# Sixteen cache copies moved among the weight pieces of the first stage of a hybrid decoder step

## What is computed

```python
u = x * (1 + sc1) + sh1
proj = u @ w_in                       # 1024 x 2560, float32
xa, ga, q, k, v = jnp.split(proj, [D_A, 2 * D_A, 2 * D_A + D_B, 2 * D_A + 2 * D_B], axis=-1)
y_a, new_conv, h_last = rglru_branch(xa, ga, ...)
q = rope(q.reshape(b, t, N_HEADS_B, HEAD_DIM), pos)
k = rope(k.reshape(b, t, N_HEADS_B, HEAD_DIM), pos)
...
k_all = jnp.concatenate([k_buf.astype(k.dtype), k], axis=1)      # the 8 sequences
v_all = jnp.concatenate([v_buf.astype(v.dtype), v], axis=1)
keep = min(WIN_MAX, k_all.shape[1])
new_k, new_v = k_all[:, -keep:], v_all[:, -keep:]
```

## Time and profile before

| | us |
|---|---|
| median of three runs | 1359.38 |
| lowest, highest | 1357.69, 1365.87 |
| profiled execution, span | 1363.8 |
| TensorE busy (PE) | 1196.5 (88%) |
| VectorE busy (DVE) | 735.4 (54%) |
| ScalarE busy (ACT) | 577.3 (42%) |

### The profile page before, as it was taken

How to read it: one execution, slowest core, us unless ns; L and a number is a source line. 1 busy time by engine, 2 the same in 40 slices (tenths; PEclk the granted TensorE clock), 3 DMA queues, 4 the chain that set the end, 5 groups by cost and what they waited for, 6 DMA issues and landing times. The chain is left out here.

```text
span 1363.8 us, 20897 instructions
## 1 busy us (share of the span) xinstructions
PE 1196.5 (88%) x6933; PEld 907.3 (67%) x6934; DVE 735.4 (54%) x1247; ACT 577.3 (42%) x845; POOL 137.3 (10%) x129
## 2 busy tenths in 40 slices
PE   5699899999699979969995389999999999999854
PEld 3699787877255647627783277777778877778721
DVE  3356534343356747527545775789641455476147
ACT  2556443111245644214233264677531454465124
POOL 0000000000000001002431200011000000000055
PEclk8799899999699999879997599999999999999977
DMA  9985931259669948877333596899661455597184
GB/s 333 368 289 195 354 126 64 70 179 333 242 206 352 307 134 273 272 208 233 126 119 130 183 335 261 324 380 399 232 234 62 138 215 210 214 371 268 38 342 178
DMA packets 102028, 316.94 MB, mean 232 GB/s; under 512 B 12845, under 2 KB 21533, under 8 KB 95290
## 3 DMA queue, kind: packets, MB, share of 16 engines
q1 hardware_dynamic: 85146, 273.97, 57.5%
q0 software_dynamic: 6432, 23.33, 4.8%
q10 hardware_dynamic: 10384, 18.76, 3.7%
HBM read 281.22 MB, written 101.93 MB: 281 GB/s over the span
## 5 line engine op out<-in xcount | busy, mean ns | idle before, releaser
L2584 DVE TENSOR_TENSOR e_downl<-e_wd,e_downh 128x1024 fp32r<-128x1024 f32 x64 | 74.1, 1220 | 65.3 <-ACT e_downh L2479 65.3
L2646 PE MATMUL e_psY<-e_downh,e_hTh 128*128 128x512 f32 x216 | 91.0, 421 | 15.7 <-DVE e_hTl L2605 14.5
L2479 ACT CAST e_downh<-e_wd 128x1024 fp32r<-128x1024 f32 x64 | 62.4, 1048 | 68.5 <-DMA e_wd<-in_w_exp_down 68.5
L552 PE MATMUL n_psA<-n_wh,u_h 128*128 128x512 f32 (+1 forms) x216 | 88.1, 408 | 0.4 <-DVE n_wl L811 0.4
L2646 PE MATMUL e_psG<-e_gateh,e_xTh 128*128 128x512 f32 x216 | 86.4, 400 | 2.0 <-DVE e_gatel L2578 2.0
L2646 PE MATMUL e_psG<-e_uph,e_xTh 128*128 128x512 f32 x216 | 87.8, 406 | 0.2 <-issue 0.2
L2648 PE MATMUL e_psG<-e_gatel,e_xTh 128*128 128x512 f32 x216 | 85.9, 398 | 0.0
L2647 PE MATMUL e_psG<-e_gateh,e_xTl 128*128 128x512 f32 x216 | 85.9, 398 | 0.0
L554 PE MATMUL n_psA<-n_wh,u_l 128*128 128x512 f32 (+1 forms) x216 | 85.8, 397 | 0.0
L2647 PE MATMUL e_psY<-e_downh,e_hTl 128*128 128x512 f32 x216 | 85.7, 397 | 0.0
L2648 PE MATMUL e_psY<-e_downl,e_hTh 128*128 128x512 f32 x216 | 85.5, 396 | 0.0
(11 more groups left out here) (406 smaller groups left out, 2573.0 us busy)
## 6 DMA issues: line engine op xcount, KB each, us to landing
e_wg<-in_w_exp_gate SPq DMA_DIRECT2D x16, 2048.0 KB
e_wu<-in_w_exp_up SPq DMA_DIRECT2D x16, 2048.0 KB
e_wd<-in_w_exp_down SPq DMA_DIRECT2D x16, 2048.0 KB, 14.4
out_k_s<-in_cache_win_k SPq DMA_DIRECT2D x8, 4088.0 KB, 21.1
out_v_s<-in_cache_win_v SPq DMA_DIRECT2D x8, 4088.0 KB, 34.5
a_wring<-in_w_ada SPq DMA_DIRECT2D x16, 1024.0 KB, 5.3
scratch_y<-e_y ACTq DMA_DIRECT2D x54, 256.0 KB, 4.3
n_wr<-in_w_in SPq DMA_DIRECT2D x20, 512.0 KB, 7.0
```

The lines of the kernel that those rows point to most:

```text
L552: nc.tensor.matmul(dst, lh, rh, start=(k == 0), stop=False)
L2479: nc.scalar.copy(w["down"][H_][:, k, :], ew["down"][:, k, :]).then_inc(s_dh.sem, s_dh.unit)
L2584: nc.vector.tensor_tensor(w["down"][L_][:, k, :], ew["down"][:, k, :], w["down"][H_][:, k, :], ALU.subtract).then_inc(s_dl.sem, s_dl.unit)
L2646: nc.tensor.matmul(dst, left[H_], right[H_], start=first, stop=False)
```

## The change

All sixteen copies are issued in `front`. One each stands behind p2, p3, p6, p8, p9, p10, p11, p12 and p13, two behind p5, four behind p15; the last one is issued once the nine k tiles are transposed, ahead of the small result writes as before. `attention` issues no copies and waits only for the two small writes of new rows. `finish` waits for 16 copies in place of 12.

```diff
-            finish(nc, a, out, dram, ident, route, tables, s_tables, s_cache, 12)
+            finish(nc, a, out, dram, ident, route, tables, s_tables, s_cache, 2 * B)
...
-    COPIES = (2, 3, 4, 5, 7, 8, 10, 11)
-    LAST = 4
+    COPIES = {2: 1, 3: 1, 5: 2, 6: 1, 8: 1, 9: 1, 10: 1, 11: 1, 12: 1, 13: 1, 15: 4}
+    LAST = 1
...
             for n in range(RAW, NPIECE):
                 load_piece(n)
-                if n in COPIES:
+                for _ in range(COPIES.get(n, 0)):
                     copy_cache(copied)
                     copied += 1
             sp.wait_ge(s_qt.sem, s_qt.at(NTT))
             for _ in range(LAST):
                 copy_cache(copied)
                 copied += 1
+            assert copied == 2 * B
...
-            def copy(b):
-                sp.dma_start(ov[b:b + 1, 0:PAST - TS, :], cv[b:b + 1, TS:PAST, :]).then_inc(s_cp.sem, s_cp.unit)
...
-            copy(CT)
-            copy(CT + 1)
             sp.wait_ge(s_mm.sem, s_mm.at(PIECES))
...
-            copy(CT + 2)
-            copy(CT + 3)
...
-            sp.wait_ge(s_cp.sem, s_cp.at(B - CT + 2))
+            sp.wait_ge(s_cp.sem, s_cp.at(2))
```

More of the change, by code:

```diff
@@ L1049, in attention @@
         turned = lambda s: 2 * chunk0[s]
-        cv = a["cache_win_v"].rearrange("b s h d -> b s (h d)")
         ok, ov = (out[n].rearrange("b s h d -> b s (h d)") for n in ("k_s", "v_s"))
```

## The result

The changed kernel takes 1367.71 us (median of 10 runs, 1363.65 to 1369.25), the kernel before 1361.55 us (median of 10 runs, 1350.12 to 1365.87). The medians lie 6.2 us apart. The ratio estimated from all the runs is 1.0056, 95% interval 1.0036 to 1.0076: 7.6 us slower (4.9 to 10.3), inside what the prediction called within 1%. The forecast was +1.6 us and 1361. The span of the profiled execution went from 1363.8 to 1367.5 us, +3.7.

What follows compares the result with a forecast made beforehand. TensorE, busy for 88% of the span, was taken to bound the kernel. The shift up to the squares +1.2, the expensive step +6.0 and the block end −5.6 gave +1.6 us on the median 1359.4: 1361.0 us, range 1353 to 1371.

Steps and rivals of the forecast that it cites:

- The block end: First stage's end: late copies delay the small result writes that TensorE's next block awaits; moving three copies earlier gives −5.6 us.
- The copies leave attention at no price: Attention stage: taking out its four 4 MB copies is worth 0, since nothing waits for them before 505.5.
- The landing of the weight pieces: First stage's DMA queue: p9 lands at 138.2, p11 at 165.1, p13 at 194.4, p16 at 265 (256.6 to 272.7).
- the second rival: First stage: V copies at 13.3 us and stores paid in full, p16 at 272.7, sum +9.3, 1368.7 us; chance 0.17.
- the third: First stage: V copies cost 14.6 us each, stores in full, p16 at 281.8, sum +18.4, 1377.8 us; chance 0.08.
- the K price with the stores in full: Queue up to p16: copies at 12.1 us each plus 7.7 us for stores, landing p16 at 264.3.
- The squares: Sum of squares before gate r3: TensorE waits until about 182.9, then 2 us of slow clock; shift up to here +1.2 us.
- i2's wait and its gain: Gate matmuls for channel block 2: p9 lands earlier, the wait goes, TensorE gains 7.4 us, which does not last.
- the chain: From p11's landing through ScalarE and VectorE to the sum of squares: moves by 0.3 us alone, TensorE starting 0.8 us earlier.
- The expensive step: Copies and stores ahead of p16: it lands at 265, TensorE stalls 4.0 us at the fifth k tile, plus 2 us half clock.
- A clock that stays up into attention is no rival: Block end into attention: the clock drops within the first microsecond after the last transposes, so a shorter gap gains nothing there.
- a shorter attention as a sign against itself: Attention from its first matmul (349.0 to 510.7) should stay unchanged; getting shorter without its copies would show the forecast wrong.

Runs made afterwards that it cites:

- the spread copies: Changed kernel with twelve copies in the first stage (none behind p10, two behind p15, none at the end) and four in attention: 1348.14 us, ratio 0.9907.

## Why the prediction was right or wrong, point by point

**The block end: right.** Foreseen −5.6 us, some 1.4 us left; the wait fell from 7.26 to 1.55, −5.7. The copies leave attention at no price, right too (157.9 us with four, 157.9 without, both with the same clock at the start).

**The landing of the weight pieces: right, all of them.** p9 foreseen at 138.2, taken at 138.92; p11 165.1, taken at 165.97; p13 194.4, taken at 194.81, and r3 did not wait for it; p16 at 265.0. The last was issued at 232.9:

```profile
L373 SPq DMA_DIRECT2D n_wr<-in_w_in x1: 374/374/374, 232.9 to 232.9; - x1
...
DMA to landing us min/median/max: 31.4/31.4/31.4
```

It landed at 264.3. So the copies cost 12 to 13.4 us each in the queue, and the second rival (the V price and the stores in full) and the third (dearer copies) did not come. What the 11 stores took from the queue is not told apart: 264.3 is also what the prediction has for the K price with the stores in full. The Trainium skill (DMA: Bandwidth & Descriptors, "Issuing engines are not separate DMA queues"), which the prediction held against the change, agrees with the trace in that the two queues share the engines (96 packets of each in 16 us); what that cost here was the latency of the stores, and the forecast asked only for their bytes.

**The squares: right place, one term too small.** i2's wait and its gain (7.4) went, the wait came at 183: foreseen until 182.9, measured until 183.81, the start of this line before (183.77). The slow clock behind it was charged 2.0 us; the row 183.81 alone takes 3.76 in place of 1.99, and the v matmuls run at half clock until 191.5. From the squares to r3 are 16.76 us after and 13.16 before: 3.6 us. The shift at r3 is +3.6, not +1.2: 0.9 from the chain, 1.6 from the clock. The price came from one row, that of i2 (1.95 us behind a wait of 5.47); at the two new waits it was 3.6 us behind 8.25 and 1.8 us behind 9.03, so one row was no bound for it.

**The expensive step: the failed one.** The prediction put the stall at the fifth k tile, behind p16's cast, 4.0 + 2 us. It came at the third, 9.03 us long, with 1.8 us of slow clock behind it (14.4 − 3.6 − 9.0), and by then p16's cast held nothing: ScalarE took p16 and p17 at 268.26, when the store had let TensorE go on; p16 had been there since 264.3 (232.9 + 31.4). The false step is the sentence that charges each v and k store "between 0 and 0.7 us". It asked what the stores take from the copies' queue, and not what the copies do to the stores: it had no landing time for a store and named nobody who waits for one. The wait was in the code, the third rotation waiting for the first store because ROT is 2; before, with landings of 2.0 us, it never showed in the trace. The runs with a third buffer and with 2 KB pieces show that the store is what TensorE waited for. The foreseen stall came only in the latter, where p16 was 6.4 us later still (270.7). With the landing and the shift that the changed kernel had, the prediction's own working gives it almost nothing: 264.3 + 6.0 = 270.3 for the rotated tile against 265.83 + 3.6 = 269.4 for TensorE, 0.9 us, and with a third buffer it was nil.

**"A clock that stays up into attention is no rival": wrong in this execution.** Granted clock in attention's first stretches, before and then after:

```profile
349.00:354.00 5.00, 2.73 (x12) 1.44 (x12) 1.36 (x9) 1.37 (x6) 1.39 (x3) 0.50 0.74 241
354.00:359.00 5.00, 4.23 (x16) 0.99 (x14) 2.90 (x12) 1.36 (x5) 0.00 (x0) 0.50 0.94 313
359.00:364.00 5.00, 5.00 (x25) 2.28 (x17) 0.88 (x3) 1.95 (x6) 0.00 (x0) 0.50 0.99 385
```

```profile
357.70:362.70 5.00, 2.03 (x12) 1.04 (x12) 1.36 (x9) 1.37 (x6) 1.40 (x3) 0.61 0.70 231
362.70:367.70 5.00, 4.18 (x17) 1.05 (x16) 2.90 (x12) 1.36 (x5) 0.00 (x0) 0.71 0.98 331
367.70:372.70 5.00, 5.00 (x40) 2.70 (x40) 2.88 (x9) 2.42 (x7) 0.00 (x0) 1.00 1.00 406
```

Before, the clock is at 0.50 for attention's first 15 us; after, it falls only behind the first matmuls (0.93 us in place of 1.65) and is back at 1.00 ten microseconds in: the 3.8 us. The prediction read 0.67 in the gap as what any gap does. But the shorter gap alone does not settle it: with the same 1.55 us, attention took 157.3 to 157.9 us in three of the profiles, 158.8 to 159.9 in four (one of these with 4.2 us for the late bias), and 161.0 with the spread copies. The first matmuls' row tells them apart: 0.93 us in the changed kernel, with a third buffer, with four copies back in attention (157.3 to 157.9) and with the small writes ahead (159.5); 1.11 with 2 KB pieces (158.8); 1.65, like the kernel before, without copies, with the copy behind p10 moved and with the spread copies (159.2 to 161.0). Why the clock falls ahead of the first matmul in the last three is left open; against the 161.7 of before, the profiles with the short gap give back between 0.7 and 4.4 us. The prediction had named a shorter attention as a sign against itself. It came, but not for want of the copies: with four of them back attention took the same 157.9 us.

**The sum.** Foreseen +1.2 + 6.0 − 5.6 = +1.6. Measured in the two profiles to the start of sampling: +3.6 + 10.8 − 5.7 − 3.8 = +4.9. Two terms too small (2.4 and 4.8 us), one gain that was ruled out (3.8). That the range held the time is in part luck, these errors offsetting one another: the place and the cause of the largest term were wrong.

## What to carry to other kernels

Ask of every DMA on a queue beside bulk copies not only what it takes from them, but when it will land and who waits for that: list the buffers that its completion frees, though the trace shows no wait there today. Bulk copies belong where neither a weight piece behind them on their own queue nor a small transfer on another has a reader or a buffer waiting. Here the order that kept to this was 12.6 us faster than the kernel before, which held a weight piece and the block end, and some 20 us (by the ratios) faster than the changed kernel, which held a weight piece and a store, with not a byte less moved. And a stall on TensorE costs more than its length: here 1.8 to 3.6 us of half clock on top of waits of 5 to 9 us.

## What the runs showed of the hardware

In the changed kernel a 256 KB store on one queue took 10 to 45 us to land beside 4 MB copies on another queue, 2 us alone, and up to 7 us when the copies went in 2 KB pieces. With fewer copies beside them v stores landed in between: 2 to 15 us with four copies back in attention, 7 to 29 with the spread order. The engines took as many packets from one queue as from the other (96 and 96 in 16 us; 92 and 87 in 1 us with 2 KB pieces), whatever a packet held. An estimate from the first pair: 96 packets of copies in 16 us are 6 on each of 16 engines, 2.7 us each; a store of 128 packets of 2 KB gives each engine 8; if each of these waits for one copy packet, the store takes 8 × 2.7 = 21 us. The v stores of that stretch landed at 206.8, 229.8 and 252.7, 23 us apart. ScalarE issued a new one every 5.6 to 7.3 us, so the queue fell behind, and the first k store came to stand behind four v stores. The Trainium skill (DMA: Bandwidth & Descriptors, "Queues, rings and completion order") says that a DMA engine takes turns between its queues a whole packet at a time; the packet counts above agree with that. That each single packet of a store waits for one of a copy was not followed packet by packet.

The fine pieces had a price, which the expectation had named as possible: with 2 KB pieces p11, p13 and p16 came 3 to 6 us later than with the same copies in 65 KB packets, though from 200 to 240 us nearly the same was moved (361 and 342 GB/s in the two halves, 378 and 328 in the changed kernel). Whether that is the copies' own rate or the stores taking their share earlier was not told apart. A third candidate is SP itself: its eight issues of the last four copies took from 203.54 to 252.53 us, and p16 was issued at 252.58 in place of 232.89.
